# Counting on ScalarE: the wide comparisons of a prompt's threshold search split between two engines, and three key gathers issued further ahead

## The reference

```python
def indexer_topk(q_idx, w_idx, k_idx, q_pos, n_keep):
    s = jax.nn.relu(jnp.einsum('bqhd,bld->bqhl', q_idx, k_idx))
    score = jnp.einsum('bqhl,bqh->bql', s, w_idx) * IDX_SCALE
    score = jnp.where(key_pos[None, None, :] <= q_pos[None, :, None], score, -jnp.inf)
    _, idx = lax.top_k(score, n_keep)          # prompt: n_keep = 132 of 528; decode: 256 of 4100
    return idx
...
def sparse_attention(q, k_sel, v_sel, key_pos, q_pos, rel_bias):
    ...
    logits = jnp.einsum('bqhd,bqkhd->bqhk', q, k_sel) * ATTN_SCALE + bias
    logits = jnp.where((rel >= 0)[:, :, None, :], logits, -jnp.inf)
    p = jax.nn.softmax(logits, axis=-1)
    return jnp.einsum('bqhk,bqkhd->bqhd', p, v_sel)
```

## Time and profile before

| | us |
|---|---|
| median of 3 runs (1318.24 to 1332.81) | 1327.62 |
| the profiled execution, its own time | 1326.33 |
| its span, first to last instruction | 1324.5 |
| TensorE busy | 1169.9 (88%) |
| VectorE busy | 782.5 (59%) |
| ScalarE busy | 267.3 (20%) |
| GpSimd busy | 185.0 (14%) |

### The profile page before, as it was taken

One profiled execution on the slowest core, in us unless ns is written; L12 is line 12 of the kernel. 1 busy time (PEld: TensorE's weight loads), 2 busy tenths in 40 slices (PEclk: granted clock), 3 DMA queues, 4 the chain that ended last, 5 costly groups with the idle time before them and its releaser, 6 DMA issues. The chain is left out here.

```text
span 1324.5 us, 16619 instructions
## 1 busy us (share of the span) xinstructions
PE 1169.9 (88%) x6671; PEld 916.7 (69%) x6671; DVE 782.5 (59%) x1622; ACT 267.3 (20%) x526; POOL 185.0 (14%) x202
## 2 busy tenths in 40 slices
PE   6999989999987986741877999999999999989996
PEld 3478778854645752310434557889999999989995
DVE  5108999478888988969973122126766665551220
ACT  2110121132111012110222310222332222141120
POOL 0001200000000121057476400000000000000112
PEclk9869999999998998875667889999999999999998
DMA  8110424021033552147477534102233323222330
GB/s 262 48 50 1 165 75 163 32 80 65 19 127 107 202 178 62 40 130 218 143 241 244 175 72 136 26 0 64 76 85 96 94 67 96 76 72 79 102 105 26
DMA packets 109494, 135.68 MB, mean 102 GB/s; under 512 B 8117, under 2 KB 76109, under 8 KB 108372
## 3 DMA queue, kind: packets, MB, share of 16 engines
q1 hardware_dynamic: 92085, 80.70, 20.1%
q0 software_dynamic: 13824, 46.91, 11.3%
q10 hardware_dynamic: 3509, 7.01, 1.5%
HBM read 129.06 MB, written 5.54 MB: 102 GB/s over the span
## 5 line engine op out<-in xcount | busy, mean ns | idle before, releaser
L1173 PE MATMUL G<-xnH,whi 128*128 128x274 f32 x704 | 205.2, 291 | 0.7 <-DVE aext L1701 0.7
L1174 PE MATMUL G<-xnL,whi 128*128 128x274 f32 x704 | 203.5, 289 | 0.0
L1175 PE MATMUL G<-xnH,wlo 128*128 128x274 f32 x704 | 202.9, 288 | 0.0
L1174 PEld LDWEIGHTS G<-xnL,whi 128*128 128x128 f32 x704 | 133.4, 189 | 0.1
L1173 PEld LDWEIGHTS G<-xnH,whi 128*128 128x128 f32 x704 | 132.4, 188 | 1.0 <-issue 0.9
L1175 PEld LDWEIGHTS G<-xnH,wlo 128*128 128x128 f32 x704 | 133.1, 189 | 0.0
L1660 DVE TENSOR_TENSOR wlo<-wraw,whi 128x2048 fp32r<-128x2048 f32 (+1 forms) x38 | 76.4, 2011 | 92.0 <-ACT whi L2033 91.3
L726 PE MATMUL G<-xnT,wring 128*128 128x280 f32 x512 | 125.8, 406 | 0.5 <-ACT wB L1803 0.5
L706 PE MATMUL G<-wring,xnT 128*128 128x512 f32 (+1 forms) x208 | 103.1, 653 | 17.6 <-DVE stat L1568 14.4
L726 PEld LDWEIGHTS G<-xnT,wring 128*128 128x128 f32 x512 | 97.8, 194 | 24.8 <-ACT wB L1803 1.2
L1173 PE MATMUL G<-hfH,whi 128*128 128x274 f32 x352 | 102.9, 292 | 0.0
(11 more groups left out here) (364 smaller groups left out, 1859.6 us busy)
## 6 DMA issues: line engine op xcount, KB each, us to landing
wraw<-in_w_up_dram SPq DMA_DIRECT2D x44, 512.0 KB, 5.2
wring<-in_w_in_dram SPq DMA_DIRECT2D x9, 2048.0 KB, 8.0
wraw<-in_w_down_dram SPq DMA_DIRECT2D x16, 704.0 KB, 4.4
qB<-scr_q SPq DMA_DIRECT2D x32, 256.0 KB, 3.6
wring<-in_w_in_dram ACTq DMA_DIRECT2D x2, 2048.0 KB, 9.7
wring<-in_w_o_dram SPq DMA_DIRECT2D x2, 2048.0 KB, 8.4
toep<-scr_toep SPq DMA_DIRECT2D x1, 2432.0 KB, 14.7
wring<-in_w_in_dram SPq DMA_DIRECT2D x2, 1024.0 KB, 9.3
```

Of the source, the lines that this page charges most:

```text
L1173: pe.matmul(out, w_hi, x_hi, start=start, stop=False)
L1174: pe.matmul(out, w_hi, x_lo, start=False, stop=False)
L1175: return pe.matmul(out, w_lo, x_hi, start=False, stop=stop)
```

## The change

Units of a step now run in the order r = 4, 3, 2, 1. In 25 of the 33 steps (0 to 2 and 11 to 32) the two wide units, r = 4 and r = 3, are a plain comparison on VectorE, which leaves zeros and ones in a tile, and ScalarE adds up the tile by an ACTIVATE with an accumulator (`counts`). VectorE waits for both sums after the step's last unit. ScalarE's program gets these counts at fixed places. The copy of the turned token lists (`tokT`) moves from behind the eighth `gb` gate to ahead of the fourth. GpSimd issues the gathers of keys 12 to 14 ahead of its wait for tile 4's key projection. Some semaphores are merged, which changes no wait.

```diff
+    UNIT_ROWS, COUNTED = (4, 3, 2, 1), (4, 3)
+    COUNTED_STEPS = [i for i in range(COMPARE + 1) if i < 3 or i >= 11]
+    COUNTS_BY = [(12, 13), (15, 17), (19, 21), (23, 25)]
...
-                i, r = units[0] // 4, 1 + units[0] % 4
+                i, r = units[0] // 4, UNIT_ROWS[units[0] % 4]
...
-                step(dve.tensor_scalar(out[r][0:rows, 0:seen], sel[0:rows, r - 1, NS:NS + seen], thr, None,
-                                       op, ALU.add, accum_out=cntP[0:rows, r - 1:r]), free=r < NT - 1)
+                x, made = sel[0:rows, r - 1, NS:NS + seen], out[r][0:rows, 0:seen]
+                if r in COUNTED and i in COUNTED_STEPS:
+                    step(dve.tensor_scalar(made, x, thr, None, op), S["compare_made"], free=True)
+                else:
+                    step(dve.tensor_scalar(made, x, thr, None, op, ALU.add, accum_out=cntP[0:rows, r - 1:r]), free=r != UNIT_ROWS[-1])
+                if r != UNIT_ROWS[-1]:
+                    continue
+                if i in COUNTED_STEPS:
+                    dve.wait_ge(S["compare_counted"], len(COUNTED) * (COUNTED_STEPS.index(i) + 1))
...
+        def counts(upto):
+            for m in range(counted[0], sum(i < upto for i in COUNTED_STEPS)):
+                i = COUNTED_STEPS[m]
+                for n, r in enumerate(COUNTED):
+                    _, rows, seen, _ = att_tile(r)
+                    act.wait_ge(S["compare_made"], len(COUNTED) * m + n + 1)
+                    x = buffer_of(i, r)[0:rows, 0:seen]
+                    step(act.activation(x, x, ACT.Copy, accum_out=cntP[0:rows, r - 1:r]), S["compare_counted"], free=True)
+                counted[0] += 1
+        counts(1)
         pair_in("q", 0)
+        counts(2)
         pair_in("k", 0)
+        counts(3)
         gate("gb", 0)
...
         for n in range(1, KM):
+            if n == 3:
+                act.wait_ge(S["tok_turned"], 1)
+                step(act.activation(tokT[:, :], TB[0:2 * NS, 1, 256:256 + P], ACT.Copy), S["tok_done"], free=True)
             gate("gb", n)
...
         for r in range(1, NT):
+            counts(COUNTS_BY[r - 1][0])
             pair_in("q", r)
             if r >= 2:
                 probs_in(2 * r - 4)
+            counts(COUNTS_BY[r - 1][1])
             pair_in("k", r)
...
         pair_out(NT - 1)
         take_pair(NT - 1)
+        counts(COMPARE + 1)
...
-        for i in range(9, 12):
+        for i in range(9, 15):
             keys(i)
         ready(pool, ("k", NT - 1))
...
         for i in range(7):
-            keys(12 + i)
+            keys(15 + i)
             values(2 + i)
-        for i in range(19, 25):
+        for i in range(22, 25):
             keys(i)
```

More of the change, by code:

```diff
@@ L463, in build_in @@
         aext_clear xn2_done fst_ready fst_done fst_loaded ua_in ua_conv ua_silu xres_loaded y_trans y_nat tail_trans
[L464 removed]
+        tail_done dv_own act_own kin_done q_dup newsc_done pair_ready pick_ready pages_done
         relpad_done prompt_mask newhot_loaded f_high f_split xn2_val xn2_high hf_high hf_split dn_half
[L466 removed]
+        relpad_loaded dve_tap dec_done win_ready kw_loaded qis_clear compare_made compare_counted""".split()
     S = {n: sem(n) for n in names}
@@ L556, in build_in, with buffer_of @@
     COMPARE = 32
+    UNIT_ROWS, COUNTED = (4, 3, 2, 1), (4, 3)
+    COUNTED_STEPS = [i for i in range(COMPARE + 1) if i < 3 or i >= 11]
+    EARLY_UNITS = 12
+    COUNTS_BY = [(12, 13), (15, 17), (19, 21), (23, 25)]
+    def buffer_of(i, r):
+        first = len(UNIT_ROWS) * i + UNIT_ROWS.index(r)
+        return (compared if first < EARLY_UNITS else compared_late)[r]
     Q_FILL = 4
@@ L923, in _ @@
         pe.wait_ge(S["newsc_done"], 1)
-        pe.matmul(TB[:, 0, 0:NS], C("place", NS), newsc[:, :], start=True, stop=True).then_inc(S["newcol_ready"], 1)
+        pe.matmul(TB[:, 0, 0:NS], C("place", NS), newsc[:, :], start=True, stop=True).then_inc(S["newsc_ready"], 1)
         fill(6)
@@ L974, in _ @@
         fill(IN_L + 1)
-        pe.wait_ge(S["diag_ready"], 1)
-        pe.matmul(TB[:, 1, 64:64 + 2 * NS], ones[0:NS, :], diag, start=True, stop=True).then_inc(S["bcast_ready"], 1)
+        pe.wait_ge(S["pair_ready"], 2)
+        pe.matmul(TB[:, 1, 64:64 + 2 * NS], ones[0:NS, :], diag, start=True, stop=True).then_inc(S["pick_ready"], 1)
         fill(IN_L + 4)
@@ L1373, in _ @@
         norm_take(1)
-        dve.wait_ge(S["newcol_ready"], 1)
+        dve.wait_ge(S["newsc_ready"], 2)
         step(dve.tensor_scalar(segS[:, 1024:], TB[:, 0, 0:NS], C("unplaced"), None, ALU.add), S["seg_done"])
@@ L1418, in prompt_units @@
                 of = bestP if i == COMPARE else trialP
-                if r == 1 and 1 <= i < COMPARE:
+                if r == UNIT_ROWS[0] and 1 <= i < COMPARE:
                     step(dve.tensor_scalar(trialP, bestP, 1 << (31 - i), None, ALU.bitwise_or))
-                elif r == 1 and i == COMPARE:
+                elif r == UNIT_ROWS[0] and i == COMPARE:
                     step(dve.tensor_tensor(bestP, bestP, belowP, ALU.add))
@@ L1424, in prompt_units @@
                 thr = 0.0 if i == 0 else of[0:rows, r - 1:r].bitcast(F32)
-                step(dve.tensor_scalar(out[r][0:rows, 0:seen], sel[0:rows, r - 1, NS:NS + seen], thr, None,
-                                       op, ALU.add, accum_out=cntP[0:rows, r - 1:r]), free=r < NT - 1)
-                if r == NT - 1 and i == 0:
+                x, made = sel[0:rows, r - 1, NS:NS + seen], out[r][0:rows, 0:seen]
[7 more added lines that the diff above has]
+                    dve.wait_ge(S["compare_counted"], len(COUNTED) * (COUNTED_STEPS.index(i) + 1))
+                if i == 0:
                     step(dve.tensor_scalar(posP, cntP, float(KEEP_PROMPT), None, ALU.is_ge), free=True)
@@ L1430, in prompt_units @@
                     step(dve.tensor_scalar(bestP, belowP, 31, None, ALU.logical_shift_left))
-                elif r == NT - 1 and i < COMPARE:
+                elif i < COMPARE:
                     step(dve.scalar_tensor_tensor(keptP, cntP, float(KEEP_PROMPT), posP, ALU.is_ge, ALU.is_equal))
                     step(dve.scalar_tensor_tensor(bestP, keptP, 31 - i, bestP, ALU.logical_shift_left, ALU.bitwise_or))
-                elif r == NT - 1:
+                else:
                     step(dve.tensor_scalar(needP, cntP, -1.0, float(KEEP_PROMPT), ALU.mult, ALU.add))
@@ L1482, in _ @@
         step(dve.tensor_scalar(diag[:, 0:NS], ident[0:NS, 0:NS], thr32, None, ALU.mult))
-        step(dve.tensor_scalar(diag[:, NS:], ident[0:NS, 0:NS], need32, None, ALU.mult), S["diag_ready"])
+        step(dve.tensor_scalar(diag[:, NS:], ident[0:NS, 0:NS], need32, None, ALU.mult), S["pair_ready"])
         new_in, at32, cum32, m32 = newsc[:, :], newm[:, 0:NS], newm[:, NS:2 * NS], newm[:, 2 * NS:]
@@ L1488, in _ @@
         prompt_units(2, compared)
-        dve.wait_ge(S["bcast_ready"], 1)
+        dve.wait_ge(S["pick_ready"], 2)
         step(dve.tensor_copy(thr_need, TB[:, 1, 64:64 + 2 * NS]))
@@ L1933, in _ @@
                     take_value(r)
+        counted = [0]
+        def counts(upto):
[8 more added lines that the diff above has]
+        counts(1)
         pair_in("q", 0)
+        counts(2)
         pair_in("k", 0)
+        counts(3)
         gate("gb", 0)
@@ L1945, in _ @@
                 act.dma_start(ring(i, k, m), parts[0][2]).then_inc(w_loaded[i % 2], 16)
-        act.wait_ge(S["tok_turned"], 1)
-        step(act.activation(tokT[:, :], TB[0:2 * NS, 1, 256:256 + P], ACT.Copy), S["tok_done"], free=True)
         act.wait_ge(S["new_lg"], 1)
```

4 lines of the change are left out of this document (1 added, 3 removed).

## The result

The changed kernel takes 1315.67 us (median of 20 runs), the one before 1326.50 (20 runs, in which the three of the first table are included). The ratio is 0.9915, with a 95% interval from 0.9891 to 0.9939: 11 us faster, or 8 to 14. The profiled execution took 1318.84 us with a span of 1317.0 us.

What follows compares the result with a forecast made beforehand. VectorE sets the end in the list stage and behind round 4, TensorE's projections with pair_norm in the rounds. Terms -1.2, -8.5 and -1 sum to -10.7 us: 1317 against 1327.62, range 1304 to 1328.

Steps and rivals of the forecast that it cites:

- the -1 for the attention: Behind the mask: reordered gathers fill GpSimd's 9.61 us pause at keys 19 with three values; 1 us off, between 0 and 3.
- the prediction's own last sign: Mask 10 us earlier but the end not: then the attention has its own clock or gathers to wait for.
- A step, 2.48 us: One whole counted search step: 2.48 us instead of 2.88, saving 0.40, with ScalarE slower than VectorE by a little.
- the first rival: Counted steps: plain comparisons are slow, 0.72 us for 528 columns, so only 5.3 us gained, 1322 us; chance 0.15.
- List stage, -1.2: Steps 0 to 2, counted while ScalarE is idle, save 0.4 us each, 1.2 us in all.
- Steps 3 to 12 and the token copy, nothing: Round 1: reordered or counted steps and the earlier tokT copy bring nothing, as TensorE's key projection waits for weights.
- Rounds, 0: Rounds 2 to 4: counting only shortens VectorE's waits at pair_norm, leaving half a microsecond of slack each; 0 us gained.
- Behind round 4, -8.5: From round 4 to the first mask: -7.4 for key waits, +1.7, -3.6 for steps, +0.8; together 8.5 us off.
- step 25's late sum: Start of the stretch behind round 4: counts cannot begin before ScalarE has turned tile 4; 1.7 us lost.
- The +0.8 for slower comparisons beside gathers: Behind round 4: some comparisons stretch by 0.2 us while GpSimd issues gathers; 0.8 us lost.
- forecast of a mask at 610 to 611 us: End of TensorE's wait for selb: the wait falls from 39.8 to about 30 us, with the mask at 610 to 611.
- The rival in which the clock turns the gain round: Attention: half of the 72 us at 2.4 GHz is granted 1.2, costing 30 us more, 1347 us; chance 0.06.

Runs made afterwards that it cites:

- the first comparison: The changed kernel against the kernel before, 20 runs each on a chip not known: 1315.67 against 1326.50 us, ratio 0.9915.
- TensorE kept busy: The changed kernel plus 11 unread 128x128 products for each of the search's last eight steps ahead of the first mask: ratio 0.9896 to the kernel before.
- The gathers alone: The kernel before with only the gathers of keys 12 to 14 moved ahead of the token lists, run twice: ratios 0.9994 and 0.9998.

## Why the prediction came out right, step by step

The predicted time, 1317, is 1.3 above the median measured, and up to the mask the mechanism is the one forecast. That it is so near is luck in part: the -1 for the attention was not earned, and the same two kernels gave -10.8 us in the first comparison and -14.4 on chip 2. It is also the luck of the chip. On chips 0, 1 and 6 the early gathers brought the mask forward by as much and the time did not follow, which is the prediction's own last sign, that the attention may have its own gathers to wait for. By terms:

- **A step, 2.48 us.** 2.54, with the 0.2 us wait for ScalarE at its end. The 718 ns row that priced the first rival is not the price of the new comparison: 44 of them in two shapes average 491 and 456 ns, beside GpSimd's gathers too (the last section has what goes with the 718). By the rule of the Trainium skill (VectorE: DVE Perf Modes, the perf-mode tier table) the sum was mine. The trace agrees, with 491 ns for 528 columns, where the comparison that also sums takes 750.
- **List stage, -1.2.** -1.22, in every kernel with two tiles counted.
- **Steps 3 to 12 and the token copy, nothing.** The four traces of before and changed give 83.2 and 82.0 against 80.9 and 80.5 us. The 1.9 between the means is the landing of the weights: in all four, TensorE's key projection of tile 1 starts only when they are there, 11.65 and 10.53 us behind their issue before, 9.31 and 8.87 in the changed kernel. So the first wait for `natsq` read 2.49 and 2.05 us, not 3 to 4. The early copy makes the small product wait 0.88 us less for `tokT`, and 2.04 us between the last gate product and the query projection became 1.29. This hides under the weights, as forecast. With the old gap the query projection would have ended 9.1 us behind the issue, so the copy brought 0.3 us at the most. In the six traces of kernels with the early copy on chips 0, 1 and 6 the gap is 2.17 to 2.23 us, so there it brought nothing. And the stretch varies more than this: with TensorE kept busy, which is the changed kernel up to here, it took 86.2 us.
- **Rounds, 0.** The waits 0.34, 0.34 and 0.38, where 0.45, 0.4 and 0.5 were worked out; 82.7 and 81.8 us before, 82.9 and 81.9 changed.
- **Behind round 4, -8.5.** 39.0 and 38.8 became 30.1 and 30.0: -8.9. The gathers alone gave -7.5 (7.4 expected), step 25's late sum cost 1.69 (1.7), and 23.5 us with that sum on VectorE and two products fewer fits the same count. The +0.8 for slower comparisons beside gathers was the term mis-sized: -7.4 + 1.7 - 3.6 is -9.3, which leaves 0.4. Hardly any comparison was stretched; in the trace of the changed kernel one of the 44 was, by 0.1 (a pair of 0.96 us at 578.04, where the others take 0.87).
- **The attention, -1.** 118.7 and 120.3 before, 119.9 and 117.9 changed: -0.6 between the means, where two traces of one kernel lie 1.6 and 2.0 apart. The reason given was wrong too. Three values were to fill GpSimd's pause at keys 19, but they stand behind keys 19 in the new order, and the pause grew from 9.61 to 13.69 us. It ends 15 us behind the mask in both kernels.

```profile
619.85 1.99 POOL L2175 DMA_INDIRECT ksel<-in_cache_k_dram,gather_row x1 [13.69 <-DVE lgat L1605]
```

The terms as measured, -1.2, -8.9 and at most -0.3, give -10.1 to -10.4; the two comparisons measured -10.8 and -14.4 by their medians.

The pair of traces shown moved only 7.5 us, though the mask came 16.1 earlier by the clock on the wall. 3.8 of the 16.1 was an earlier start and 2.3 the earlier landing of the weights. Both are chance, and the forecast of a mask at 610 to 611 us missed its 604.95 by them. Another 1.2 went between the mask and the 48-row tile, and 7.4 from there on, where the same TensorE instructions ran at the other level. First before, then changed, the 48-row tile's transposes and products:

```profile
763.34 0.55 PE L1017 MATMUL UB<-pack,pr 48*128 48x48 f32 x5
763.82 1.06 PE L1001 MATMUL G<-kT,qT 64*48 64x512 f32 x2
```

```profile
747.99 0.74 PE L1026 MATMUL UB<-pack,pr 48*128 48x48 f32 x5
748.66 1.94 PE L1010 MATMUL G<-kT,qT 64*48 64x512 f32 x2
```

TensorE is busy without a gap in both; the two products take 1.06 us at 2.4 GHz and 1.94 at 1.2. From its first to its last such product the tile takes 29.6, 29.6 and 28.1 us where the last three of its eight heads run at 2.4 GHz (both traces of before, the second of the changed kernel) and 33.4 us in the first trace of the changed kernel and in the one with TensorE kept busy, which had 120.2 us to that tile like the others; from there to the end these two need 3.6 to 4.8 us more. That is two values 7.4 to 9.8 us apart, and the changed kernel itself shows both, so it is no fixed cost of the change; whether it is more frequent with the change five traces cannot tell. The rival in which the clock turns the gain round named the right place but a price of 30 us.

## What to carry to other kernels

Read first who waits at the end of each stretch: 14 of the 25 steps made faster stood in front of a wait and gave nothing, while three gathers moved past a queue gave most of what was won up to the mask. Whether that reaches the end of the program depended on the chip. Split work between two engines step by step only until the helper's chain is as long as the owner's own work; here one more tile of 352 columns made the step slower than no help. And compare traces between common events, since a start 4 us off and a clock level worth 8 are as large as the change.

## What the runs showed of the hardware that I had not expected

Executions of the same kernel came in two kinds: 1326 to 1327 us on chip 2 and in the first comparison, 1351 on chips 0, 1 and 6, 1.8% apart. On the three, ScalarE, VectorE and TensorE stand still in the attention for 3 to 22 us at a time with no event that ends it. All these waits begin while GpSimd still issues gathers (DMA share 0.4 to 1.0 in all but one), and kernels that took 217.5 to 234.9 us from the start of the list stage to the mask gave ratios from 0.993 to 1.000 in another order. And the same 2 MB of weights, issued at the same place, landed after 8.8 to 11.6 us in five traces.

The traces tie the 718 ns of the earlier trace rows to the issue of a gather on GpSimd. The comparison of 528 columns in the last mask takes 0.72 us where it starts 0.49 us into such an issue (first pair, kernel before), and 0.48 us where it starts 0.27 us into one (second pair, first run of gathers only):

```profile
682.62 0.72 DVE L1467 TENSOR_SCALAR late<-sel,bits 48x528 f32<-48x528 f32 x1
682.13 0.95 POOL L2139 DMA_INDIRECT ksel<-in_cache_k_dram,gather_row x1 [0.31 <-issue]
```

```profile
687.31 0.48 DVE L1467 TENSOR_SCALAR late<-sel,bits 48x528 f32<-48x528 f32 x1
687.04 0.95 POOL L2139 DMA_INDIRECT vsel<-in_cache_v_dram,gather_row x1 [0.30 <-issue]
```

The 14 traces have 28 such comparisons of 480 or 528 columns in the masks. The 16 that start 0.48 to 0.63 us into an issue take 0.58 to 0.72 us, and end 0.2 to 0.3 us behind it; the 12 that start earlier in an issue, or beside none, take 0.46 to 0.48.
